# A two-layer transformer trunk with product-key expert lookup on one core: the order of row slots and the place of projection work in each layer's opening

## What is computed

```python
def peer_block(xb, w_q, sub_keys, expert_u, expert_v):      # xb: 128 tokens of 1024
    q = (xb @ w_q).reshape(T, PEER_HEADS, 2, PEER_HALF)      # 8 heads, 2 halves of 128
    s = jnp.einsum('thpd,hpkd->thpk', q, sub_keys)           # 128 keys for each half
    sv, si = lax.top_k(s, PEER_TOPK)                         # 16 of each
    cand = sv[:, :, 0, :, None] + sv[:, :, 1, None, :]       # 256 sums, of which the top 16
    top_s, pos = lax.top_k(cand.reshape(...), PEER_TOPK)
    eidx = jnp.take_along_axis(cidx, pos, axis=-1)           # row numbers of 16384 experts
    gate = jax.nn.softmax(top_s)
    act = jax.nn.gelu(jnp.einsum('thkd,td->thk', expert_u[eidx], xb))
    return jnp.einsum('thk,thkd->td', gate * act, expert_v[eidx])
```

## Time and profile before

| | us |
|---|---|
| median of 3 runs | 3377.75 (3376.77 to 3378.26) |
| the profiled execution | 3351.6 |
| its span, first to last instruction | 3349.9 |
| PE busy, mean granted clock | 2385.1 (71%), 0.862 |
| DVE busy | 2011.0 (60%) |
| ACT busy | 1063.9 (32%) |
| POOL busy | 1231.2 (37%) |
| gathers (software queue) | 1073.81 MB, 77.6% of 16 engines' span |
| chain that ended last | DMA 42%, PE 31%, DVE 6%, POOL 5%, ACT 5% |

### The profile page before, as it was taken

The page is one execution under the profiler, slowest core; times in us unless marked ns, Lnnn a source line. Parts: engine busy times, 40 slices in busy tenths (PEclk is TensorE's granted clock), DMA queues, the critical chain, the costliest instruction groups (busy, mean ns, idle before and its releaser), DMA issues.

```text
span 3349.9 us, 34887 instructions
## 1 busy us (share of the span) xinstructions
PE 2385.1 (71%) x12133; PEld 1026.4 (31%) x12133; DVE 2011.0 (60%) x4937; ACT 1063.9 (32%) x3359; POOL 1231.2 (37%) x1075
## 2 busy tenths in 40 slices
PE   8999898666766666666787796667666666677555
PEld 3554554222322232222232452323222322222101
DVE  1233524677777777675565346777777776755543
ACT  3012212343333344333222223433333343333322
POOL 1322311444444444334444113443444443444441
PEclk9999889787888887777899898888887887798877
DMA  6223143999999999999999768999999999999995
GB/s 241 76 76 113 51 163 151 385 421 420 401 422 421 421 389 418 417 417 418 421 416 419 287 233 340 421 421 411 420 421 420 392 421 419 419 407 402 418 422 210
DMA packets 192869, 1169.39 MB, mean 349 GB/s; under 512 B 20762, under 2 KB 24116, under 8 KB 60468
## 3 DMA queue, kind: packets, MB, share of 16 engines
q0 software_dynamic: 147456, 1073.81, 77.6%
q1 hardware_dynamic: 45236, 93.36, 7.6%
HBM read 1165.00 MB, written 2.10 MB: 348 GB/s over the span
## 4 chain that ended last, share of the span: by engine, by line
DMA 42%; PE 31%; DVE 6%; POOL 5%; issue 5%; ACT 5%; POOLq 0%; ACTq 0%; DVEq 0%
PE banks L747 19%; DMA scr<-in_peer_rows,idx_v 12%; PE banks L1088 11%; DMA scr<-in_expert_rows,idx_v 11%; DMA ring<-in_expert_rows,idx_v 10%; DMA ring<-in_peer_rows,idx_v 8%; POOL scr L694 3%; POOL ring L694 3%; DVE scr L2142 2%; DVE ring L2142 2%; ACT ring L1551 2%; ACT scr L1545 1%; ACT L1545 0%; ACT ring L1530 0%; ACT L1504 0%
## 5 line engine op out<-in xcount | busy, mean ns | idle before, releaser
L1088 PE MATMUL banks<-scr,ring 128*32 128x512 f32 x2064 | 645.5, 765 | 443.7 <-ACT ring L1551 435.5
L1088 PE MATMUL banks<-ring 128*32 128x512 f32 x2032 | 626.8, 749 | 406.9 <-ACT ring L1551 406.7
L2142 DVE CUSTOM_DVE_ANT_0 ring<-ring 128x1024 f32<-128x1024 f32 x382 | 468.0, 1225 | 316.1 <-DMA ring<-in_expert_rows,idx_v 161.3
L2142 DVE CUSTOM_DVE_ANT_0 scr<-scr,ring 128x1024 f32<-128x1024 f32 x386 | 472.8, 1225 | 302.7 <-DMA scr<-in_peer_rows,idx_v 154.6
L1545 ACT ACTIVATE scr<-scr 128x2 f32<-128x2 f32 x512 | 104.0, 203 | 1572.5 <-DVE scr L2142 1570.3
L694 POOL DMA_INDIRECT scr<-in_expert_rows,idx_v x258 | 281.0, 1089 | 458.5 <-PE banks L1088 350.0
L694 POOL DMA_INDIRECT scr<-in_peer_rows,idx_v x258 | 286.7, 1111 | 434.9 <-PE banks L1088 352.5
L694 POOL DMA_INDIRECT ring<-in_expert_rows,idx_v x254 | 262.4, 1033 | 412.4 <-PE banks L1088 320.5
L694 POOL DMA_INDIRECT ring<-in_peer_rows,idx_v x254 | 269.0, 1059 | 382.2 <-PE banks L1088 307.7
L747 PE MATMUL banks<-hT,scr 128*128 128x128 f32 (+3 forms) x2576 | 384.3, 310 | 17.4 <-DVE idx_v L2129 15.8
L747 PEld LDWEIGHTS banks<-hT,scr 128*128 128x128 f32 (+1 forms) x2576 | 329.2, 200 | 135.2 <-issue 103.8
(11 more groups left out here) (235 smaller groups left out, 2400.0 us busy)
## 6 DMA issues: line engine op xcount, KB each, us to landing
ring<-in_w_mod SPq DMA_DIRECT2D x12, 2048.0 KB, 8.2
ring<-in_w_in SPq DMA_DIRECT2D x7, 2048.0 KB, 12.8
scr<-in_w_in SPq DMA_DIRECT2D x5, 2048.0 KB, 27.6
scr<-in_peer_w_q SPq DMA_DIRECT2D x1, 8192.0 KB, 27.7
scr<-in_w_q SPq DMA_DIRECT2D x4, 2048.0 KB, 12.5
scr<-in_peer_rows,idx_v POOLq DMA_INDIRECT x258, 12.5
scr<-in_expert_rows,idx_v POOLq DMA_INDIRECT x258, 12.6
ring<-in_w_out SPq DMA_DIRECT2D x2, 2048.0 KB, 8.5
```

The source lines that it names most:

```text
L1088: last = nc.tensor.matmul(psum[2 + c][32 * g:32 * g + 32, :], spread[:, i % 8, :], rows[slot_of(i)][:, D + c * CW:D + (c + 1) * CW], start ...
L2142: V.tensor_tensor_reduce(u, u, xq[g], 1.0, 0.0, ALU.mult, ALU.add, dots[:, n % 2, k:k + 1]).then_inc(dotted, 1)
```

## The change

- `slot_of`: gathers 0 to 35 of a layer go round six slots, 4, 5, 6, 7, 0, 1; from gather 36 the order is that of before (slots 2, 3, 4, ...). Before, gathers 0 to 7 used 4, 5, 6, 7, 0, 1, 4, 5 and gather 8 began the round of eight at slot 6.
- PE: the second halves of tiles 1, 2 and 3 are made in two parts of four k steps each (`project_part`): tile 1 before and after add_up(2), tile 2 after batches 4 and 5, tile 3 after batches 6 and 7. Both layers share `first_sums`. In layer 1 the first halves of tiles 1 and 2 change places with quad rows.
- DVE adds these halves after dots 13, 24 and 32 (before: between dots 3 and 4, and after dots 9 and 12), and interleaves head 1's routing with dots 4 to 7. The routing has twelve parts, the gate being the last.
- Layer 0, head 0: the index is moved and packed on its own, ahead of the gate (`move_idx`, `pack_idx`, `move_gate`, `pack_gate`), and ACT takes the exponential ahead of the copies of the quad rows. `pack` now copies the index before the gate, behind the gate's semaphore.

```diff
 def slot_of(i):
-    return (4, 5, 6, 7, 0, 1, 4, 5)[i] if i < SLOTS else (i - 2) % SLOTS
+    return (4, 5, 6, 7, 0, 1)[i % 6] if i < OPENING else (i - OPENING + 2) % SLOTS
...
+                def move_idx(j):
+                    n = n0 + j
+                    pe.wait_ge(idx_expanded, n + 1)
+                    to_quads(psum[4 + n % 2][:, 0:TOPK], idx_x).then_inc(idx_moved, 1)
...
                     add_up(batch)
+                    if batch < 8:
+                        project_part(("wo", "wo2")[layer], batch // 2, w, batch % 2)
...
+            def project_part(name, t, w, part):
+                o = begin(name, t, 1) if part == 0 else psum[jobs.bank[jobs.number(name, t, 1)]]
+                for k in range(KT // 2 * part, KT // 2 * (part + 1)):
+                    last = mm(o[:, :], yT[:, k, t * P:(t + 1) * P], w[1][:, k, :], k, KT)
+                if part == 1:
+                    last.then_inc(bank_ready, 1)
+
+            def first_sums(name, w, scores_q, scores, move, add_up):
+                scores(1)
+                add_up(0)
+                scores(2)
+                move(1)
+                add_up(1)
+                project_part(name, 1, w, 0)
+                scores_q(3)
+                add_up(2)
+                project_part(name, 1, w, 1)
+                add_up(3)
...
                 quad_rows(0, 0, 0, 0)
+                move_idx(0)
                 quad_rows(0, 0, 1, 2)
-                move(0)
+                pe.wait_ge(idx_packed, 1)
+                move_gate(0)
                 pe.wait_ge(xq_set, 2)
...
                 scores_out(0)
+                softmax_exp(0)
                 quads_out(0, 0, 0)
                 quads_out(0, 1, 2)
-                softmax_exp(0)
                 quads_out(0, 2, 2)
...
+            def first_units(scores_out, softmax_exp, unit, q_out):
+
                 scores_out(1)
                 unit(0)
+                scores_out(2)
                 softmax_exp(1)
-                scores_out(2)
                 unit(1)
...
-            def first_heads(layer, name, pack, route_all, dots_of):
+            def first_heads(layer, name, tiles, pack, route_parts, dots_of):
                 dots_of(0, 4)
-                add_projection(layer, name, 3, (0,))
-                route_all(1)
-                add_projection(layer, name, 1, (1,))
-                dots_of(4, 8)
+                for t in tiles:
+                    add_projection(layer, name, t, (0,))
+                for i in range(4):
+                    route_parts(1, 3 * i, 3 * i + 3)
+                    dots_of(4 + i, 5 + i)
                 pack(1)
...
-                route_all(0)
+                route_parts(0, 0, ROUTE_PARTS - 1)
+                pack_idx(0)
+                route_parts(0, ROUTE_PARTS - 1, ROUTE_PARTS)
                 add_projection(0, "wo", 2, (0,))
-                pack(0)
-                first_heads(0, "wo", pack, route_all, dots_of)
+                pack_gate(0)
+                first_heads(0, "wo", (3,), pack, route_parts, dots_of)
...
-            beside = {9: lambda: add_projection(0, "wo", 2, (1,)), 12: lambda: add_projection(0, "wo", 3, (1,)),
+            beside = {13: lambda: add_projection(0, "wo", 1, (1,)), 24: lambda: add_projection(0, "wo", 2, (1,)),
+                      32: lambda: add_projection(0, "wo", 3, (1,)),
```

More of the change, by code:

```diff
@@ L1103, in next_quads @@
                         quad_rows(layer, t, g, 6)
-                start(scores_q, scores, move, add_up)
+                w = start(scores_q, scores, move, move_idx, move_gate, add_up)
                 for batch in range(4, N_BATCH):
@@ L1125, in peer, with start_first @@
                     add_up(batch)
+                    if batch < 8:
+                        project_part(("wo", "wo2")[layer], batch // 2, w, batch % 2)
                     if batch in beside:
                         beside[batch]()
[L1129 to L1133, removed]
+            def project_part(name, t, w, part):
[15 more added lines that the diff above has]
+                add_up(3)
+            def start_first(scores_q, scores, move, move_idx, move_gate, add_up):
+                w = [use_chunk("w_out", CW * n) for n in range(2)]
+                empty(pe, "yT", KT - 2)
+                empty(pe, "yT", KT - 1)
                 project("wo", 0, w)
@@ L1151, in start_first @@
                 project("wo", 3, w, (0,))
[L1152 to L1162, removed]
+                first_sums("wo", w, scores_q, scores, move, add_up)
+                return w
             def mix_products(o, w, c0, tokens):
@@ L1219, in late_cols, with start_second @@
                 last.then_inc(bank_ready, 1)
-            def start_second(scores_q, scores, move, add_up):
+            def start_second(scores_q, scores, move, move_idx, move_gate, add_up):
                 w = [chunk(chunk_number("w_o_2", CW * n)) for n in range(2)]
@@ L1264, in start_second @@
                 quad_rows(1, 0, 3, 0)
+                project("wo2", 2, w, (0,))
                 project("wo2", 3, w, (0,))
                 empty(pe, "cvL")
[L1267 to L1277, removed]
+                first_sums("wo2", w, scores_q, scores, move, add_up)
+                return w
             def p_cols(k):
@@ L2109, in route @@
                                         ).then_inc(idx_expanded, 1)
+                    if part == 11:
                         dve.wait_ge(exp_done, n + 1)
@@ L2115, in route, with route_parts, pack_idx, pack_gate @@
                                                ALU.mult, ALU.mult).then_inc(gate_expanded, 1)
[L2117 to L2118 removed]
+                def route_parts(j, first, last):
+                    for part in range(first, last):
                         route(j, part)
[L2121 removed]
+                def pack_idx(j):
                     n = n0 + j
[L2124 to L2125 removed]
+                    dve.wait_ge(idx_moved, n + 1)
                     if n >= IDX_HEADS:
                         dve.wait_ge(summed, (n + 1 - IDX_HEADS) * TOPK)
[L2128 to L2129 removed]
+                    V.tensor_copy(idx_v[:, n % IDX_HEADS, :], psum[4 + n % 2][:, 0:TOPK]).then_inc(idx_packed, 1)
+                def pack_gate(j):
+                    n = n0 + j
+                    dve.wait_ge(gate_moved, n + 1)
+                    V.tensor_copy(gate_v[:, n % IDX_HEADS, :], psum[4 + n % 2][:, TOPK:2 * TOPK]).then_inc(gate_packed, 1)
+                def pack(j):
+                    dve.wait_ge(gate_moved, n0 + j + 1)
+                    pack_idx(j)
+                    pack_gate(j)
                 def dot(i):
@@ L2152, in dots_of @@
                         j, part = divmod(i + 16, 12)
-                        if i >= 8 and j < N_HEADS and part < ROUTE_PARTS:
+                        if i >= 8 and j < N_HEADS:
                             route(j, part)
```

59 lines of the change are left out of this document (23 added, 36 removed).

## The result

| | kernel before | changed kernel |
|---|---|---|
| median | 3377.75 us | 3359.94 us (3356.28 to 3362.90) |
| ratio, with its 95% interval | | 0.9946 (0.9935 to 0.9957) |
| the profiled execution, its span | 3351.6, 3349.9 | 3356.28, 3354.5 |

The change saves 17.8 us where 37.9 were forecast, and 3359.94 us lies 2 us above the range. One execution of the kernel with parts of one matmul took 4440.88 us and is left out of that kernel's figures. Different experiments ran on different chips, each beside the kernel before; across them the ratios are compared.

The account below looks back on a forecast made before the run. Gathers of 1 MB rows set the pace, with time lost where DMA idles in both layers' openings. Gains of 22.4 (layer 0) and 17.5 (layer 1) less 2 give 37.9 us off 3377.75: 3340 us, range 3322 to 3358.

Parts of the forecast that it names:

- rival (c): Slower by PE's clock: parts at 1.2 GHz (7.1 us) lose 33 us a layer; 3404 us; chance 0.04.
- The remaining quads took 4.86 us after that idle gap and take 3.70 without it: Layer 0, head 0: quads end at 528.1 instead of 531.3, so PE work behind them comes 3.1 us earlier.
- At 24 for about 4 us: DVE after dot 24 queues behind PE's part for about 4 us; dots 25 to 27 and routing parts wait.
- batch 6 loses about 3: Layer 0: batch 6 loses about 3 us with DVE's wait at dot 24; gather 36 lands near 635.
- Adding 0.9 for DVE's wait at dot 32: Layer 0: with 0.9 us added, the stream runs on as if row 36 had landed at 635.8, before 658.2.
- below 5 us: Sign in the trace after: row 36's wait stays below 5 us.
- Layer 1, 17.5 us: Layer 1's opening, same form as layer 0's: row 36 at 2072.0 instead of 2089.5, a gain of 17.5 us.
- The baseline: Profiled execution 3351.6 us, median 3377.75; the 26 us unplaced, gain taken off the median; profiled execution should read near 3314.
- (b): Six slots leak: batches 3 to 7 lose 1 us a pair, 20 us in all; gain 18, 3360 us; chance 0.15.
- (a): Nothing leaks: six slots carry the full rate from gather 12 on; gain 50 to 60, 3323 us; chance 0.10.
- (d): It doesn't tell: old stall moves to gather 36, or gain is lost later; 3372 to 3384 us; chance 0.05.
- POOL waits more than 5 us again and again between gathers 18 and 36: Sign that would show the forecast wrong: repeated POOL waits above 5 us between gathers 18 and 36.

Follow-up runs that it names:

- parts of one matmul: Changed kernel with three of the four matmuls of every part left out in both layers: 3347.43 us, ratio 0.9901.
- hold three: Changed kernel with gathers 1 to 3 of layer 0 waiting for PE's last quad row, gather 0 going as before: 3351.45 us, ratio 0.9920.
- the late index and the hold: Changed kernel with head 0's index and gate moved together again and gathers 1 to 3 waiting for PE's last quad row: 3358.24 us, ratio 0.9948.
- the adds moved: Changed kernel with DVE's three adds of second halves after dots 16, 27, 35 instead of 13, 24, 32, both layers: 3349.77 us, ratio 0.9906.
- the two profiles: The changed kernel profiled twice; gather 0 to gather 511 of layer 1 took 1352.7 and 1356.1 us.
- the second profile: The kernel before, unchanged, profiled again for an execution near its median: 3373.5 us, span 3371.7.
- the last kernel: Changed kernel with gathers 1 to 3 of layer 0 held for PE's last quad row and adds after dots 16, 27, 35: 3345.34 us, ratio 0.9904.

## Why the prediction was wrong

**Right.** The bound (gathers in the openings) and the slot order: gather 12 left its 21 us wait in both layers, and six slots don't leak in themselves. Gather 0 at 2.6 us behind the mark, forecast 2.8. The parts run at full rate (3.70 for 3.57; one of the six took 4.41). The DMA share of 575 to 630 was 0.87, forecast above 0.85. The direction, and that rival (c) would not come: PE's clock in 595 to 650 rose from 0.72 to 0.90.

**Wrong, term by term.** The forecast had gather 60 of layer 0 at 164.0 behind the mark; it went at 182.1, 18.1 us late. Of this 6.1 arose before gather 4, 2.2 from there to gather 12, -2.6 up to 18, 11.6 from 18 to 36 and 0.8 after.

- *"The remaining quads took 4.86 us after that idle gap and take 3.70 without it"*: PE stood 3.93, because the same edit had sent the first four gathers out beside the first set, and after that stand they took 5.53. The step costed the edit on PE and on POOL, and never asked what the earlier transfers would meet. With the hold the step's sum came out within 0.2 us. In the earlier trace rows the quad rows ran beside the first gathers and lost nothing but the cold start; with the late index and the hold they took 4.87 us as there, in the three disturbed traces with index and gate moved together 8.2 to 8.3, so the profile had caught an undisturbed execution.
- *"At 24 for about 4 us"*, *"batch 6 loses about 3"*: the wait was 5.60, and gather 30 waited 12.07. The prediction listed dots and routing as queued behind DVE's add, and left out the pack of head 2, for which PE itself waits. That is 5 us at gather 30. With the adds moved, 18 to 36 took 52.6 us, with the hold as well 50.8, forecast 48.6, instead of 60.2: in those two traces 7.6 and 9.4 of the 11.6 are gone, and by the spread between executions of one order these differences are rough.
- *"Adding 0.9 for DVE's wait at dot 32"*, row 36's wait *"below 5 us"*: DVE waited 5.27 us for the last part and gather 36 waited 9.44. It waited 5.9 to 10.7 us for that part in both layers of every kernel with parts; no experiment was made on it, and what it costs stays open.
- *Layer 1, 17.5 us*: 14.0 and 10.6 in the two profiles. The circle is there as well (8.98 us before gather 30); the rest was not followed up, and its cause stays open.
- *The baseline*: the profile's 26 us under the median lay for the most part in a faster stream (5.6 us from gather 60 on in layer 0, 9.4 in the same stretch of layer 1, against the second profile) and in an opening without the disturbance. The gain was taken off the median, which was right (the profiled execution of the changed kernel read 3356.28, not near 3314), but an undisturbed opening was taken for the usual one.

**The rivals.** (b), six slots leak, had the right time (3360) by luck and in the main the wrong mechanism: the loss isn't one microsecond in every pair but sits for the most part at gathers 4 and 30. Of the 15.6 us by which gathers 18 to 36 exceed eighteen times 2.48, 9.3 lie between 28 and 30, 2.5 before and 3.7 behind. (a) didn't come. Of (d) the late last part did, 9.44 us before gather 36, but not a DVE wait of 16.56 us. "POOL waits more than 5 us again and again between gathers 18 and 36" came true in part (5.73 before gather 20, 12.07 before 30, 9.44 before 36).

By the Trainium skill, "DMA: Bandwidth & Descriptors", Anatomy of one DMA, a 1 MB gather takes an estimated 4.4 us, which gave six slots 1.4 us more slack. The traces don't agree: gather 0 of hold three, with no other beside it, took 5.81 us from its issue at 523.66 to its dot at 529.47, like the row's 5.77. With 24.8 us for ten gathers in the last kernel there was nothing left there for more slack to win.

## What to carry to other kernels

When a wait is placed on an engine, list every semaphore that the instructions behind it raise, and look whether the engine being waited for needs one of them: an add put ahead of such a pack cost 5 us in layer 0. When transfers are started earlier, look at what short instructions run beside them; holding gathers 1 to 3 back 5 us let gather 4 go 6 us earlier. And profile each kernel twice before reading differences of a few microseconds.

## What the runs showed of the hardware

When gathers 0 to 3 of 1 MB each went out one behind the other beside PE's quad rows, PE's short records came in pieces with gaps of 0.3 to 1.0 us ("issue"), in nine traces of ten. In the six of them with the early index ACT and DVE took note of finished products 3 to 4 us late ("remote"). In the three others 128 quad records took 8.2 to 8.3 us (526.45 to 534.69 above), against 4.86 and 4.87 after the same stand without the disturbance. Gather 0 alone did nothing of the kind (hold three), and once the four were under way neither did they: 128 records ran without a gap at a DMA share of 1.01, in 5.53 us with the granted clock at 0.50 for the first 3.3 of them. What the start of the gathers shares with the other engines the traces don't show. A gather with no other beside it took 5.81 us from issue to dot.

The stream of gathers itself differs between executions: 2100 to 3300 ran at 416 GB/s in the first profile of the kernel before and at 412 in the second, and from gather 60 to gather 511 the first profile was 15 us shorter in the two layers together (5.6 and 9.4).
